# ScalarE in place of GpSimd for the rounding of the middle groups' weights, with VectorE's order changed and the first middle group written out

## The chip, the cores and the metric

The kernel runs on one core of a Trainium2 chip. The metric is the device time of one execution in microseconds (us); the median of three executions is shown, and one more was taken with the hardware profiler. The engines are TensorE (PE, its weight loads PEld), VectorE (DVE), ScalarE (ACT), GpSimd (POOL) and SyncE (SP), which here only issues transfers. All matrices are float32, and each float32 product is made of three passes over two rounded parts (a "high" and a "low" part, both of type float32r).

## The reference, cut to what matters

Two layers work on 1040 tokens (16 of them meta tokens) of width 1024. Each layer is a mixer and then a squared-ReLU MLP with a hidden width of 4096; the change touches only the MLP.

```
def squared_relu_mlp(h, w_up, w_down):
    return jnp.square(jax.nn.relu(h @ w_up)) @ w_down

for l in range(DEPTH):
    mix = hybrid_mixer(rmsnorm(h, norm_mix_pre[l]), w_in[l], ..., w_out[l])
    h = h + rmsnorm(mix, norm_mix_post[l])
    ff = squared_relu_mlp(rmsnorm(h, norm_mlp_pre[l]), w_mlp_up[l], w_mlp_down[l])
    h = h + rmsnorm(ff, norm_mlp_post[l])
return h[:, N_META:]
```

## The kernel before, in words

The hidden width is cut into eight groups of 512. Group 0 and group 7 are computed plainly: four hidden tiles, then eight output tiles. The six groups between them (1 to 6, the middle groups) use Strassen's scheme (in Winograd's form) on 2 x 2 blocks: seven products instead of eight for the up matrix (the **up half** of a group), then seven for the down matrix (the **down half**). The fourteen weight operands of a group are either a quarter of the loaded weights (A11, A12, A22) or a sum of quarters (S1 to S4). In the code they are `UP_A11, UP_S1, UP_S2, UP_S4, UP_S3, UP_A12, UP_A22` and `DN_S4, DN_S3, DN_A11, DN_S1, DN_S2, DN_A12, DN_A22`, and TensorE multiplies them in this order. TensorE's products of the up half are called `UP_1, UP_5, UP_6, UP_3, UP_7, UP_2, UP_4`, those of the down half `X_B22, X_T3, X_B11, X_T1, X_T2, X_B21, X_T4` after their activation operand.

Each weight operand takes these steps. SP loads a quarter of 512 KB into one of four raw buffers (`raws[0..3]`, shown in traces as `w_raw` and `r`), as soon as VectorE has finished with the operand that used the buffer (`when_split`). VectorE makes sums in place (`weights_sum`, L2249). GpSimd rounds the buffer into the high part of one of three weight slots (`rounded`, L679, 128 x 1024 elements; the slots are `w_hl` twice and `w_third`), and VectorE makes the low part (`weights_low`, L2260), after which TensorE may use it.

Beside that, in each middle group, ScalarE copies four up products out of PSUM (`copied`, L1630), squares four hidden quarters (L1634) and rounds the seven activation operands (`high`, L1645); VectorE adds up products (`up_sum`, L2278), applies ReLU and the row scale (`relu`, L2283 and L2360), makes differences (L2287) and low parts of activations (`low`, L2291), and adds down products from PSUM into the output (`add_part`, L2305). SP and ScalarE both issue loads of precomputed activation sums (`t_load`, L543 and L1619; `X<-t_mem`, `t_extra<-t_mem`).

Every engine runs its instructions in the order in which they are written, and waits on semaphores; nothing is scheduled by a tool. In layer 0 a down product has four jobs (tile by tile), in layer 1 two; a job that reuses a PSUM pair waits until VectorE has added the job that was there, and the jobs in the pairs 0 and 2 of layer 0's first down product wait for the last ReLU.

Two more places matter. In group 0, VectorE copies each finished output tile to Y (`down_sum`, L2243), and between two of them makes the second half of the activation sums (`x_sums(1)`, L2437 and L2430; `x_low`, L2447), which ScalarE stores. And at the step from group 0 to group 1, SP loads the quarter A22 of group 1 after group 0's last product, since its buffer lies in the memory of group 0's hidden activations; VectorE then makes two differences on Y (L2465) and the first sum `first_up_sum`.

## Time and profile before

| quantity | value |
|---|---|
| median of 3 runs | 2308.47 us (2308.43 to 2313.3) |
| profiled execution, its time | 2309.11 us |
| profiled execution, its span | 2307.4 us |
| TensorE busy, share of the span | 97% |
| VectorE busy | 72% |
| ScalarE busy | 30% |
| GpSimd busy | 27% |
| mean granted TensorE clock | 0.992 |

The span is the time from the first to the last instruction; 1.7 us lie around it. A busy share tells how much of the span an engine was at work, and not whether its waits matter; the granted clock is 1.0 at 2.4 GHz and 0.5 at 1.2 GHz.

### The profile page before, as it was taken

To read this page: it belongs to the slowest core of one execution; us is meant where nothing else is said; L and a number is where in the kernel's file an instruction comes from. 1 tells how busy PE (TensorE), PEld (TensorE's weight loads), DVE (VectorE), ACT (ScalarE), POOL (GpSimd) and SP (SyncE) were. 2 spreads that over 40 slices of the span, in tenths; PEclk is the share of its full clock that TensorE was granted. 3 is DMA by queue.
4 is the path that set the end of the run, shared out by engine and by line. 5 is a ranking of instruction groups with operands and counts; after the bars stand their busy time and mean duration, and the time that the engine had idled before them with its cause. 6 is when DMAs were issued, how large, how long until landed. Compare 5 with 4: busy or idle time off the path is not lost.

```text
span 2307.4 us, 34577 instructions
## 1 busy us (share of the span) xinstructions
PE 2231.9 (97%) x13856; PEld 2019.0 (88%) x13856; DVE 1651.9 (72%) x1638; ACT 697.7 (30%) x828; POOL 624.5 (27%) x387
## 2 busy tenths in 40 slices
PE   7999999998999999999999999999989999999997
PEld 6999989998999999999989999877777777787787
DVE  6788644665868877977587887354768779778868
ACT  4564433340211211221254653242512112211212
POOL 3333215023222222122414432151232222222240
PEclk9999999999999999999999999999999999999998
DMA  4111002355543554542241111022556544653514
GB/s 136 33 58 39 29 26 89 92 192 209 206 175 136 204 183 155 183 171 77 83 140 46 51 37 37 20 94 80 201 185 225 187 180 152 227 182 122 196 56 146
DMA packets 122673, 290.73 MB, mean 126 GB/s; under 512 B 9552, under 2 KB 29264, under 8 KB 122576
## 3 DMA queue, kind: packets, MB, share of 16 engines
q1 hardware_dynamic: 50032, 153.30, 19.4%
q10 hardware_dynamic: 72544, 136.06, 16.9%
q8 instruction: 70, 1.15, 0.2%
q14 instruction: 27, 0.22, 0.0%
HBM read 251.25 MB, written 38.08 MB: 125 GB/s over the span
## 4 chain that ended last, share of the span: by engine, by line
PE 72%; DVE 14%; issue 5%; DMA 5%; ACT 2%; POOL 1%; DVEq 0%; SPq 0%; POOLq 0%; ACTq 0%
PE banks L802 30%; PE banks L1072 17%; PE banks L1042 9%; PE banks L933 5%; PE banks L854 2%; DMA w_raw<-w_units 2%; DMA r<-w_units 2%; DVE w_hl L2260 2%; POOL w_hl L679 1%; PE banks L857 1%; DVE hid L2278 1%; DVE sum_lo L2291 1%; PE banks L842 1%; PE banks L841 1%; PE banks L1172 1%
## 5 line engine op out<-in xcount | busy, mean ns | idle before, releaser
L802 PE MATMUL banks<-X,w_hl 128*128 128x348 f32 (+2 forms) x3744 | 648.8, 332 | 2.3 <-ACT ki L1558 1.8
L802 PEld LDWEIGHTS banks<-X,w_hl 128*128 128x128 f32 x3744 | 605.7, 188 | 30.2 <-issue 7.5
L1072 PE MATMUL banks<-sum_hi,w_hl 128*128 128x260 f32 (+1 forms) x1440 | 317.4, 325 | 24.4 <-DVE sum_lo L2291 20.0
L1042 PE MATMUL banks<-X,w_hl 128*128 128x260 f32 (+1 forms) x1944 | 316.6, 322 | 7.4 <-DVE w_hl L2260 7.4
L1042 PEld LDWEIGHTS banks<-X,w_hl 128*128 128x128 f32 x1944 | 281.4, 190 | 37.8 <-issue 8.0
L654 POOL TENSOR_SCALAR w_hl<-w_raw 128x1024 fp32r<-128x1024 f32 x70 | 91.7, 1310 | 789.9 <-issue 528.3
L1072 PEld LDWEIGHTS banks<-sum_hi,w_hl 128*128 128x128 f32 x1440 | 227.1, 191 | 53.3 <-issue 26.9
L679 POOL TENSOR_SCALAR w_hl<-r 128x1024 fp32r<-128x1024 f32 x72 | 112.6, 1564 | 361.8 <-DVE r L2249 128.6
L656 POOL TENSOR_TENSOR w_hl<-w_raw,w_hl 128x1024 fp32r<-128x1024 f32 x70 | 201.9, 2885 | 5.8
L1072 PE MATMUL banks<-sum_lo,w_hl 128*128 128x260 f32 (+1 forms) x720 | 192.7, 322 | 0.0
L1630 ACT ACTIVATE hid<-banks 128x1040 f32<-128x1040 f32 (+1 forms) x48 | 49.7, 1035 | 368.8 <-PE banks L1042 368.8
L1645 ACT ACTIVATE sum_hi<-hid 128x1040 fp32r<-128x1040 f32 (+1 forms) x72 | 77.0, 1070 | 253.1 <-PE banks L1072 222.0
L2305 DVE TENSOR_TENSOR Y<-banks,Y 128x520 f32<-128x520 f32 (+1 forms) x144 | 122.0, 867 | 23.5 <-PE banks L1072 23.4
L1072 PE MATMUL banks<-sum_hi,w_third 128*128 128x260 f32 (+1 forms) x576 | 127.3, 321 | 6.4 <-DVE Y L2305 6.4
L1072 PEld LDWEIGHTS banks<-sum_lo,w_hl 128*128 128x128 f32 x720 | 120.5, 191 | 10.0
L679 POOL TENSOR_SCALAR w_hl<-w_raw 128x1024 fp32r<-128x1024 f32 x48 | 55.8, 1162 | 267.7 <-PE banks L1072 216.2
L2260 DVE TENSOR_TENSOR w_hl<-r,w_hl 128x1024 fp32r<-128x1024 f32 x72 | 100.4, 1394 | 22.6 <-POOL w_hl L679 22.6
L1634 ACT ACTIVATE hid<-hid 128x1040 f32<-128x1040 f32 (+1 forms) x48 | 51.3, 1069 | 209.3 <-DVE hid L2283 184.7
L1042 PE MATMUL banks<-X,w_third 128*128 128x260 f32 (+1 forms) x648 | 106.6, 321 | 0.8 <-DMA X<-t_mem 0.6
L1072 PEld LDWEIGHTS banks<-sum_hi,w_third 128*128 128x128 f32 x576 | 90.1, 188 | 16.1 <-DVE Y L2305 7.7
L1042 PEld LDWEIGHTS banks<-X,w_third 128*128 128x128 f32 x648 | 92.4, 188 | 12.1 <-DMA X<-t_mem 2.7
L2249 DVE TENSOR_TENSOR w_raw<-w_raw 128x1024 f32<-128x1024 f32 x24 | 31.5, 1313 | 88.7 <-DMA w_raw<-w_units 88.6
(239 smaller groups left out, 3766.5 us busy)
## 6 DMA issues: line engine op xcount, KB each, us to landing
w_raw<-w_units SPq DMA_DIRECT2D x148, 512.0 KB, 3.5
r<-w_units SPq DMA_DIRECT2D x84, 512.0 KB, 3.8
X<-t_mem ACTq DMA_DIRECT2D x56, 520.0 KB, 6.7
X<-t_mem ACTq DMA_DIRECT2D x56, 512.0 KB, 6.7
X<-t_mem SPq DMA_DIRECT2D x16, 520.0 KB, 5.7
t_extra<-t_mem ACTq DMA_DIRECT2D x16, 520.0 KB, 7.7
X<-t_mem SPq DMA_DIRECT2D x16, 512.0 KB, 5.1
t_extra<-t_mem ACTq DMA_DIRECT2D x16, 512.0 KB, 7.1
```

What stands on the lines that cost most here:

```text
L654: nc.gpsimd.tensor_scalar(slot[:, 0], w_raw[:, s], 1.0, 1.0, ALU.mult, ALU.mult).then_inc(w_rounded, 1)
L656: nc.gpsimd.tensor_tensor(slot[:, 1], w_raw[:, s], slot[:, 0].bitcast(f32), ALU.subtract).then_inc(w_ready, 1)
L679: nc.gpsimd.tensor_scalar(wslots[W_SLOT[operand]][:, 0], raws[raw], 1.0, 1.0, ALU.mult, ALU.mult).then_inc(wpart_hi, 1)
L802: ins = nc.tensor.matmul(out[:, b, 0:t.width(b)], wp, xp[:, t.used(b)], start=first and n == 0, stop=last and n == 2)
L933: ins = nc.tensor.matmul(block_bank(j0, q)[:, 0:t.width(b)], wp, xp[:, t.used(b)], start=i == 0 and n == 0, stop=i == last_k and n == 2)
L1042: ins = nc.tensor.matmul(banks[:, first + b, 0:t.block], wp, xp[:, b * t.block:(b + 1) * t.block], start=opens and (half, kk, i) == (0, 0, ...
L1072: ins = nc.tensor.matmul(out[:, m + b, :], wp, xp[:, k, b * t.block:(b + 1) * t.block], start=k == 0 and i == 0, stop=k == 1 and i == 2)
L1630: nc.scalar.activation(by_up_blocks(l, quarter(l, q)), up_banks(l, chain), ACT.Copy).then_inc(up_copied, 1)
L1634: nc.scalar.activation(quarter(l, q), quarter(l, q), ACT.Square).then_inc(act_sq, 1)
L1645: nc.scalar.activation(sum_part(l, sum_hi, part), source, ACT.Copy).then_inc(xpart_hi, 1)
L2260: V.tensor_tensor(slot[:, 1], raws[W_RAW[operand]], slot[:, 0].bitcast(f32), ALU.subtract).then_inc(wpart_ready, 1)
L2305: ins = V.tensor_tensor(to, part_banks(l, job), to, ALU.add)
```

## The change

1. The rounding of the middle groups' weight operands moves from GpSimd to ScalarE: an ACTIVATE with `Copy` in ScalarE's own order, between its copies, squares and roundings of activations. The operands' GpSimd loop is gone; GpSimd keeps the splitting of all other weights and the zeroing of six tiles.
2. VectorE's up half: the low part of `UP_A12` stands ahead of the wait for the loads of the first down sum; ReLU 1 ahead of the wait for the load of `DN_S4`; the third up sum, the low part of `DN_S4`, ReLU 2 and the low part of `X_B22` ahead of the difference for T3.
3. ScalarE's loads for T3, T4, T2 and T1 follow the roundings that now stand ahead of them.
4. The first middle group stands outside the loop. Its A22 is loaded into a buffer of its own, `r_first`, during group 0's down half; `first_up_sum` is made ahead of group 0's last `down_sum`; the two differences on Y (`spread`) and the wait for the zeroed tiles move behind the low part of `UP_S2`.
5. `x_sums(1)` stands after group 0's second `down_sum` instead of after the first, and its low parts one `down_sum` later.

```diff
+        r_first = at("r_first", [128, 8, 128], A_T3)
...
+                sp.wait_ge(a_lo, FIRST + l * COUNTED_TILES + GT)
+                sp.dma_start(r_first[:, :, :], w_units[l, U_MLP + 8 + Q_A22]).then_inc(raw_loaded[2], 16)
...
                 sp.wait_ge(mm_done, FIRST + done(l, j_down(0, 7)))
-                raw_load(l, 1, 2, 0, Q_A22)
+                raw_load(l, 1, 3, 0, Q_A12)
                 t_load(l, 2, T2, 0)
-                raw_load(l, 1, 3, 0, Q_A12)
...
-                nc.gpsimd.tensor_scalar(wslots[W_SLOT[operand]][:, 0], raws[raw], 1.0, 1.0, ALU.mult, ALU.mult).then_inc(wpart_hi, 1)
...
+                    nc.scalar.activation(wslots[W_SLOT[operand]][:, 0], r_first[:, :, :] if first else raws[raw], ACT.Copy).then_inc(wpart_hi, 1)
...
+                    act.wait_ge(mm_done, FIRST + done(l, j_down(g - 1, 7)))
+                    rounded(g, UP_S1, first)
+                    if first:
+                        act.wait_ge(t_stored, 16 * 20 * (l + 1))
+                    rounded(g, UP_S2)
                     copied(UP_1, 0, (0, 0))
+                    rounded(g, UP_S4)
                     when_half_used(1)
                     t_load(0, T2, 1, (1,))
                     copied(UP_5, 1, (1, 0))
+                    rounded(g, UP_S3)
                     t_load(1, T3, 0)
                     when_half_used(2)
                     t_load(2, T3, 1, (1,))
                     copied(UP_6, 0, (0, 1))
+                    rounded(g, UP_A12)
+                    when_multiplied(UP_3)
+                    rounded(g, UP_A22)
                     t_load(0, T4, 0)
                     square(0, (0, 1))
                     when_half_used(3)
                     t_load(1, T4, 1, (1,))
                     copied(UP_7, 0, (1, 1))
+                    square(1, (1, 1))
+                    rounded(g, DN_S4)
+                    high(X_B22, quarter(l, (1, 1)))
                     if not last:
                         t_load(2, T2, 0)
-                    square(1, (1, 1))
-                    high(X_B22, quarter(l, (1, 1)))
+                    when_multiplied(UP_2)
+                    rounded(g, DN_S3)
+                    square(2, (0, 0))
                     high(X_T3, t3[:, :, 0:HALVES[l].width])
-                    square(2, (0, 0))
-                    square(3, (1, 0))
                     when_half_used(4)
                     when_multiplied(UP_4)
-                    for place in range(2):
+                    rounded(g, DN_A11)
+                    square(3, (1, 0))
+                    for place, (part, source, operand) in enumerate(((X_B11, (0, 0), DN_S1), (X_T1, (0, 1), DN_S2))):
+                        high(part, quarter(l, source))
+                        rounded(g, operand)
                         if not last:
                             t_load(place, T1, place)
                             continue
...
                     weights_low(g, UP_S2)
+                    if first:
+                        spread()
                     weights_low(g, UP_S4)
                     weights_low(g, UP_S3)
+                    weights_low(g, UP_A12)
                     when_loaded(g, 0, 2)
                     when_loaded(g, 1, 2)
                     weights_sum(g, SUM_DN_S1, 1, 0, 1, ALU.add)
-                    weights_low(g, UP_A12)
...
                     if m == KT - 1:
+                        first_up_sum(1, True)
                         weights_low(1, UP_A11)
                     down_sum(m, l * NJ + J_MLP, True)
-                    if m == 0:
+                    if m == 1:
                         x_sums(1)
```

The first place is VectorE in the last middle group of layer 0, from the low part of `UP_S3` (the first row) on; `w_third<-r_97` is the low part of `UP_A12`, `w_raw<-w_raw` the first down sum. Before:

```order
L2260 TENSOR_TENSOR w_hl<-w_raw,w_hl 128x1024
L2249 TENSOR_TENSOR w_raw<-w_raw 128x1024
L2260 TENSOR_TENSOR w_third<-r_97,w_third 128x1024
L2278 TENSOR_TENSOR hid_94<-banks,hid_94 128x2x520
L2283 SCALAR_TENSOR_TENSOR hid_94<-hid_94,rs 128x2x520
```

VectorE at the same place with the change:

```order
L2250 TENSOR_TENSOR w_hl<-w_raw,w_hl 128x1024
L2250 TENSOR_TENSOR w_third<-r_97,w_third 128x1024
L2239 TENSOR_TENSOR w_raw<-w_raw 128x1024
L2269 TENSOR_TENSOR hid_94<-banks,hid_94 128x2x520
L2274 SCALAR_TENSOR_TENSOR hid_94<-hid_94,rs 128x2x520
```

The low part of `UP_A12` moved from behind the down sum, which waits for two loads, to ahead of it.

The second place is VectorE around the end of the same up half, from the second up sum (`hid_95<-hid_95`) to ReLU 3 (`hid_95<-banks,rs`). Before:

```order
L2278 TENSOR_TENSOR hid_95<-hid_95 128x2x520
L2249 TENSOR_TENSOR r_96<-r_96,r_97 128x1024
L2283 SCALAR_TENSOR_TENSOR hid_95<-hid_95,rs 128x2x520
L2260 TENSOR_TENSOR w_hl<-r_96,w_hl 128x1024
L2287 TENSOR_TENSOR t_102<-hid_95,hid_94 128x1040
L2278 TENSOR_TENSOR hid_94<-banks,hid_94 128x2x520
L2291 TENSOR_TENSOR sum_lo_100<-hid_95,sum_hi_98 128x1040
L2283 SCALAR_TENSOR_TENSOR hid_94<-hid_94,rs 128x2x520
L2260 TENSOR_TENSOR w_third<-w_raw,w_third 128x1024
L2360 SCALAR_TENSOR_TENSOR hid_95<-banks,rs 128x2x520
```

VectorE at the same place with the change:

```order
L2269 TENSOR_TENSOR hid_95<-hid_95 128x2x520
L2274 SCALAR_TENSOR_TENSOR hid_95<-hid_95,rs 128x2x520
L2239 TENSOR_TENSOR r_96<-r_96,r_97 128x1024
L2269 TENSOR_TENSOR hid_94<-banks,hid_94 128x2x520
L2250 TENSOR_TENSOR w_hl<-r_96,w_hl 128x1024
L2274 SCALAR_TENSOR_TENSOR hid_94<-hid_94,rs 128x2x520
L2282 TENSOR_TENSOR sum_lo_100<-hid_95,sum_hi_98 128x1040
L2278 TENSOR_TENSOR t_102<-hid_95,hid_94 128x1040
L2250 TENSOR_TENSOR w_third<-w_raw,w_third 128x1024
L2353 SCALAR_TENSOR_TENSOR hid_95<-banks,rs 128x2x520
```

The ten instructions are the same; ReLU 1 stands one place earlier, and the third up sum (`hid_94<-banks`) two places earlier, ahead of the low part of `DN_S4` (`w_hl<-r_96`).

The third place is ScalarE at the start of the same group, from its first instruction of the group on. Before:

```order
L1630 ACTIVATE hid_94<-banks 128x2x520
L1619 DMA X<-t_mem 128x2x520
L1630 ACTIVATE hid_95<-banks 128x2x520
L1619 DMA X<-t_mem 128x2x520 x2
L1619 DMA t_extra_104<-t_mem 128x1040
L1630 ACTIVATE hid_94<-banks 128x2x520
L1619 DMA X<-t_mem 128x2x520 x2
```

ScalarE at the same place with the change:

```order
L1576 ACTIVATE w_hl<-r_96 128x1024
L1576 ACTIVATE w_third<-w_raw 128x1024
L1595 ACTIVATE hid_94<-banks 128x2x520
L1576 ACTIVATE w_hl<-r_96 128x1024
L1584 DMA X<-t_mem 128x2x520
L1595 ACTIVATE hid_95<-banks 128x2x520
L1576 ACTIVATE w_hl<-w_raw 128x1024
L1584 DMA X<-t_mem 128x2x520 x2
L1584 DMA t_extra_104<-t_mem 128x1040
L1595 ACTIVATE hid_94<-banks 128x2x520
L1576 ACTIVATE w_third<-r_97 128x1024
L1576 ACTIVATE w_hl<-r_96 128x1024
```

Six roundings (the rows with `w_hl` and `w_third`) have come between the copies and the transfers; the roundings of `UP_S3` and of `UP_A12` and `UP_A22` stand ahead of the transfers for T3 and T4.

## Rows read from the trace of the kernel before

**Rows 1.** The page: the span.
```profile
span 2307.4 us, 34577 instructions
```
**Rows 2.** TensorE's waits in layer 0's middle groups: releaser, us in total, times, longest.
```profile
PE banks L1072 <- DVE sum_lo L2291: 10.4, 6, 2.8
PE banks L1072 <- DVE Y L2305: 6.4, 6, 1.5
PE banks L1072 <- DVE hid L2360: 4.4, 4, 1.1
PE banks L1042 <- DVE w_hl L2260: 3.7, 1, 3.7
```
**Rows 3.** TensorE's waits in layer 1's middle groups.
```profile
PE banks L1072 <- DVE sum_lo L2291: 9.6, 11, 2.0
...
PE banks L1042 <- DMA X<-t_mem: 0.6, 1, 0.6
```
**Rows 4.** The chain of work in layer 0's group 4: start, us, what.
```profile
817.60 11.49 PE banks L1042 x96
...
831.78 7.44 DMA w_raw<-w_units
...
845.33 4.50 DMA r<-w_units
```
**Rows 5.** Timeline of TensorE, group 4, the start of its down half.
```profile
858.88 0.48 PE L1072 MATMUL banks<-sum_hi,w_hl 128*128 128x260 f32 x2 [1.03 <-DVE sum_lo L2291]
...
863.11 0.51 PE L1072 MATMUL banks<-sum_hi,w_hl 128*128 128x260 f32 x2 [1.11 <-DVE hid L2360]
...
868.37 0.51 PE L1072 MATMUL banks<-sum_hi,w_third 128*128 128x260 f32 x2 [0.66 <-DVE Y L2305]
```
**Rows 6.** Timeline of VectorE, group 4.
```profile
839.24 1.23 DVE L2249 TENSOR_TENSOR w_raw<-w_raw 128x1024 f32<-128x1024 f32 x1 [7.66 <-DMA w_raw<-w_units]
...
853.26 2.06 DVE L2260 TENSOR_TENSOR w_hl<-r,w_hl 128x1024 fp32r<-128x1024 f32 x1 [0.94 <-POOL w_hl L679]
855.24 1.23 DVE L2287 TENSOR_TENSOR t<-hid,hid 128x1040 f32<-128x1040 f32 x1
856.39 1.23 DVE L2278 TENSOR_TENSOR hid<-banks,hid 128x1040 f32<-128x1040 f32 x1
...
859.84 2.06 DVE L2260 TENSOR_TENSOR w_third<-w_raw,w_third 128x1024 fp32r<-128x1024 f32 x1
...
867.63 1.30 DVE L2305 TENSOR_TENSOR Y<-banks,Y 128x520 f32<-128x520 f32 x2
```
**Rows 7.** Timeline of GpSimd, group 4.
```profile
829.27 1.05 POOL L679 TENSOR_SCALAR w_hl<-w_raw 128x1024 fp32r<-128x1024 f32 x1 [2.93 <-PE banks L1042]
...
851.43 1.80 POOL L679 TENSOR_SCALAR w_hl<-r 128x1024 fp32r<-128x1024 f32 x1 [8.93 <-DVE r L2249]
```
**Rows 8.** A group of ScalarE in group 4: busy us, mean ns of one, idle before.
```profile
L1645 ACT ACTIVATE sum_hi<-hid 128x1040 fp32r<-128x1040 f32 x6 | 6.5, 1076 | 22.0 <-PE banks L1072 21.9
```
**Rows 9.** Loads of the tile X in group 4, from issue to landing.
```profile
DMA to landing us min/median/max: 3.9/6.7/8.6
```
**Rows 10.** Timeline of VectorE, from group 0 to group 1 of layer 0.
```profile
517.89 5.04 DVE L2430 SCALAR_TENSOR_TENSOR t_made<-Y,par,t_made 128x520 f32<-128x520 f32 x4
522.85 1.24 DVE L2243 COPY Y<-banks 128x1044 f32<-128x1044 f32 x1
...
554.51 1.25 DVE L2243 COPY Y<-banks 128x1044 f32<-128x1044 f32 x1 [3.34 <-PE banks L802]
...
562.59 1.21 DVE L2260 TENSOR_TENSOR w_hl<-r,w_hl 128x1024 fp32r<-128x1024 f32 x1
```
**Rows 11.** TensorE's waits over the whole span, for group 0's copies alone.
```profile
PE banks L802 <- DVE Y L2243: 4.6, 2, 2.4
```
**Rows 12.** Two stretches: us, busy times of the engines, PEclk, DMA share, GB/s.
```profile
561.00:571.70 10.70, 7.65 (x51) 7.66 (x52) 7.03 (x5) 0.53 (x2) 4.18 (x3) 0.84 0.17 52
...
1716.00:1728.50 12.50, 8.80 (x28) 6.77 (x27) 7.97 (x6) 1.14 (x2) 5.14 (x3) 0.73 0.29 99
```

More of the change, by code:

```diff
@@ L768, in _ @@
                 downs(l, 0, done(l, j_up(0, 2)), done(l, j_up(0, 3)))
-                rounded(l, 1, UP_A11, lambda: pool.wait_ge(mm_done, FIRST + done(l, j_down(0, 5))))
                 pool.wait_ge(t_stored, 16 * 20 * (l + 1))
@@ L1611, in hidden, with rounded, middle_group @@
                     nc.scalar.activation(act_hi[:, i, c], T[2 + i % 2][:, c], ACT.Copy).then_inc(a_hi, 1)
-                def middle_group(g, last):
+                def rounded(g, operand, first=False):
+                    raw, n = W_RAW[operand], groups_before(l, g)
+                    sums = {UP_S1: SUM_UP_S1, UP_S2: SUM_UP_S2, UP_S3: SUM_UP_S3, UP_S4: SUM_UP_S4,
+                            DN_S1: SUM_DN_S1, DN_S2: SUM_DN_S2, DN_S3: SUM_DN_S3, DN_S4: SUM_DN_S4}
+                    loads = {UP_A11: 1, UP_A12: 1, UP_A22: 2, DN_A11: 4, DN_A12: 3, DN_A22: 5}
+                    if operand in sums:
+                        act.wait_ge(wsum_made, WEIGHT_SUMS * n + sums[operand] + 1)
+                    else:
+                        act.wait_ge(raw_loaded[raw], 16 * (RAW_LOADS[raw] * n + loads[operand]))
+                    nc.scalar.activation(wslots[W_SLOT[operand]][:, 0], r_first[:, :, :] if first else raws[raw], ACT.Copy).then_inc(wpart_hi, 1)
+                def middle_group(g, first, last):
                     n = groups_before(l, g)
@@ L1674, in middle_group @@
                             act.dma_start(t_slot(l, place, s).bitcast(f32), b12_part(l, place, s)).then_inc(b12_loaded, 16)
-                    high(X_B11, quarter(l, (0, 0)))
-                    high(X_T1, quarter(l, (0, 1)))
                     high(X_T2, quarter(l, (1, 1)))
+                    rounded(g, DN_A12)
                     high(X_B21, quarter(l, (1, 0)))
+                    rounded(g, DN_A22)
                     high(X_T4, quarter(l, (1, 0)))
+                    if not last:
+                        when_added(6)
+                        rounded(g + 1, UP_A11)
                 w = HALVES[l].width
@@ L2321, in middle_group @@
                     when_summed(g, SUM_UP_S3)
-                    weights_sum(g, SUM_UP_S2, 0, 2, 0, ALU.subtract)
-                    weights_low(g, UP_S1)
+                    V.tensor_tensor(raws[0], r_first[:, :, :] if first else raws[2], raws[0], ALU.subtract).then_inc(wsum_made, 1)
+                    weights_low(g, UP_S1, first)
                     when_loaded(g, 3, 1)
```

101 lines of the change are left out of this document (35 added, 66 removed).

## The prediction, made before the change was run

> **What bounds the kernel now.** I read the page first: the span is 2307.4 us [rows 1], TensorE is busy for 97% of it and VectorE for 72%. So only time in which TensorE waits, or in which it runs at the lower clock, can be won. I then asked for TensorE's waits in the middle groups, because the change touches little else. In layer 0 they sum to 10.4 + 6.4 + 4.4 + 3.7 = 24.9 us [rows 2], in layer 1 to 9.6 + 3.7 + 0.6 = 13.9 us [rows 3], together 38.8 us in twelve groups. Except for 0.6 us, all of them end with an instruction of VectorE. Two more waits, 4.6 us together, one in each layer, are in group 0 on the copy to Y [rows 11].
>
> The next question is what makes VectorE late in a steady group. Take group 4 of layer 0 and count from its first product at 817.60, the group's second 0; a product takes 11.49 / 2 = 5.75 us [rows 4], so the seventh ends at 40.25. TensorE then waits 1.03 us for the low part of `X_B22`, 1.11 us for ReLU 3 and 0.66 us for an addition [rows 5]. VectorE had hardly rested just before these, but it had stood for 7.66 us up to 21.6, waiting for the load of the down quarter A22 [rows 6], which was issued at 14.2 and took 7.44 us [rows 4]. Behind this wait stood the low part of `UP_A12`, whose rounding had long been possible. Two of VectorE's operations also took 2.06 us where their like takes 1.21 [rows 6, 10], and the rounding on GpSimd beside one of them 1.80 where 1.05 is usual [rows 7].
>
> **The change, part by part.** *The rounding.* It is not in the trace on ScalarE, but ScalarE's copy of 1040 elements from SBUF into float32r is: 1.08 us [rows 8]. I take 1.05 to 1.08 for 1024. An undisturbed rounding on GpSimd is 1.05 [rows 7]. The move itself gives nothing, then; what it takes away is the stretching. In group 4 both 2.06 us operations lie in the part of VectorE's queue that TensorE waits for, and each becomes 1.22: 1.7 us. From below this is 0 (the stretching has another cause), from above 1.7; I take 1.7, since GpSimd has no instruction left in the middle groups until the last one ends.
>
> The Trainium skill, "SBUF — State Buffer", section on SBUF's two separate sides, says that VectorE's operations with two SBUF inputs and GpSimd's that read SBUF lock a shared port pair for the whole instruction and block each other. By that rule both sides' stretching goes, as in my sum; without it the 1.7 us stay.
>
> ScalarE's load is no bound: 14 roundings add 15 us to 16 us of work in a group of 84 us. But it is one queue, so I walked through it. At the group's start it rounds `UP_S1` at 0.15 and `UP_S2` at 3.1, before the copy of `UP_1` at 5.8. `UP_S4` follows at 6.9 and ends at 8.0 (TensorE needs it at 17.3). The rounding of `UP_S3` comes after the copy of `UP_5` at 11.5: 12.6 to 13.65, while GpSimd did it from 11.67 to 12.72 [rows 7]. So the low part ends at 15.0 and not 14.0, and the load of down A22 is issued at 15.1. With 7.5 us to landing it is there at 22.6. The transfers for T3, which are now issued after it was rounded (13.7 and 14.3 instead of 11.5 and 12.1), are needed at 23.0; with the median of 6.7 they land at 21.0, with the longest of 8.6 at 22.9 [rows 9]. Those for T4 move from 17.3 to about 24 and are needed at 34.5; with 8.6 they land at 33.1.
>
> *VectorE's order.* The low part of `UP_A12` now runs at 19.5, in the wait. After the landing at 22.6 there are five operations to the second up sum, which cannot start before its copy at 29.9: 22.6 + 1.25 + 1.25 + 1.15 + 1.2 + 2.4 = 29.85, just in time. Then the second up sum, ReLU 1 and the sum for `DN_S4` end at 33.6. The load for that sum is issued at 27.0 and with 4.5 us [rows 4] lands at 31.5, before it is asked for at 32.4. The third up sum waits for `UP_2`, which ends at 34.5. From here VectorE runs without a stop, an operation each 1.15 us (856.39 - 855.24) [rows 6]: the up sum at 34.6, `DN_S4` low 35.7, ReLU 2 36.9, `X_B22` low 38.0 to 39.3, the T3 difference 39.2, `DN_S3` low 40.3, ReLU 3 41.5 to 42.7, `X_T3` low 42.6, two additions 43.8, a difference 45.0, `DN_A11` low 46.15, the third addition 47.3 to 48.0. TensorE needs `X_B22` at 40.25 (1.0 to spare), ReLU 3 at 43.1 (0.4 to spare) and the third addition at 40.25 + 5 x 1.44 = 47.4: it waits 0.6. So layer 0's steady group keeps 0.6 of its 2.8 us, and the six groups 3.6 of 24.9, less the first group's start, told next. In layer 1 the same walk has 0.9 us to spare at `X_B22`, no ReLU is needed for the first product and no addition before the third, so only the 0.6 us on a load stay.
>
> *The first middle group.* TensorE waits 3.7 us there in each layer for the low part of `UP_S1`, which ends at 563.80, 9.3 us after the group's start at 554.5 [rows 2, 10]: the copy, two differences on Y, the first sum, two more sums and the rounding stand in a row. With the first sum made earlier and the differences later the row is: copy to 1.3, two sums to 3.7, low part to 4.9, and TensorE wants it at 5.75. Both waits go, and they are contained in 24.9 and 13.9. The new load of `r_first` has some ten us before anybody asks for it; what hides the differences on Y is the slack of `UP_S4`, needed only at 17.3 and now ready at 10.8. Saved in the middle groups: 24.9 - 3.6 + 13.9 - 0.6 = 34.6 us.
>
> *Group 0.* The copy to Y stands behind `x_sums(1)`, whose last four operations took 5.04 us, and starts only at 522.85 [rows 10], where the tile had been ready since 516.4. With the sums after the second copy the third is asked for at 521.9, gets its turn at about 525, and TensorE needs its banks at 527.6. Both waits go: 4.6 us [rows 11]. The stores of the sums end some 3 us later, and the loads that follow them still have over 10 us.
>
> *The clock.* The granted clock falls to 1.2 GHz after the longest waits: 0.84 over 10.7 us is 1.7 us lost at the start of group 1, 0.73 over 12.5 us is 3.4 us at layer 1's [rows 12]. In layer 0 four such stretches follow the longest waits, of 2.3, 3.7, 2.4 and 2.8 us, in layer 1 three follow those of 3.7 and 2.0 us [rows 2, 3, 11]. That is seven times 1.7 us, 11.9 us at most; since TensorE is still waiting in some of it, I take 1.5 each, 10.4 us. None followed waits of 1.0 to 1.7 us, so with 0.6 us left they should all go.
>
> The sum: 34.6 + 4.6 + 10.4 = 49.6 us. The profiled execution took 2309.1 us with 1.7 us around its span, so 2259.5; the median of the runs shown is 0.6 lower, and I predict **2259 us**.
>
> **The rivals.** *A, the walk holds*: 2259, and as its own range 2253 (the 0.6 us waits go as well, and the clock gives 11.9) to 2266 (the clock gives 7 and the waits lose a further 4). Chance 0.67.
>
> *B, part of the waits stays.* VectorE's chain has no slack at 29.9 and 1.0 us at 34.5, so a landing of down A22 after 23.6 goes through to TensorE one to one. Against it speaks that the transfers for T4 no longer share the engines with this load; for it, that layer 0's ReLU 3 has but 0.4 us. One us more in each of twelve groups is 12 us, and with one or two clock stretches left 3 us: 2274. The case that the stretching was not GpSimd's ends nearby: 1.7 us more in each of six groups is 10 us, 2269. Together 0.27.
>
> *C, the change does not do what it says*: ScalarE's rounding takes in each down product the time that the low parts had. A high part and a rounding in series end 2.2 us after the product before, and their low parts are asked for 5.75 us after it, so I see no way to this; about 2308, chance 0.02.
>
> *D, slower.* The transfers for T4 are issued 7 us later, on ScalarE's queue behind the rounding of `UP_A22`. If they landed after 34.5 + 49.6 / 12 = 38.6, 14 us after the issue, twelve waits would outweigh all gains; with 16 us it would be 12 x 1.9 = 23 us more, 2331. The longest landing in group 4 is 8.6 us [rows 9]. Chance 0.02; a further 0.02 for a slower case that I have not seen.
>
> A rule of the Trainium skill that speaks against the move is in "ScalarE: Activation LUTs", rules for kernel authors: about 0.3 us for each ACTIVATE and 0.83 ns for an element, which would be an estimate of 1.15 us a rounding. By it `UP_S3` would be 0.1 us later than in my walk and the sum 1 us smaller at most; the row of 1.08 decides.
>
> **How the numbers follow.** A has 0.67 and B 0.27; the range takes in both and reaches from **2253 to 2276**. A difference of 0.2%, 4.6 us, is about what a measurement of this kernel can tell from none. A and B lie on the faster side; C and half of the unseen are the same. Faster 0.95, same 0.02, slower 0.03.
>
> **What the profile of the changed kernel would show.** No rounding on GpSimd between group 1 and the last middle group, and ACTIVATEs of 1.05 to 1.08 us in their place; no low part over 1.3 us; a wait of VectorE for the down quarter of about 2 us after the low part of `UP_A12`; TensorE's waits in layer 0's middle groups 3 to 4 us, nearly all on an addition, in layer 1's under 1.5 us; no wait at group 1's start and in group 0; a granted clock of 1.0 from group 0 to the last middle group. I am wrong if TensorE waits on transfers for T3 or T4, if its waits on low parts stay above 1 us a group, or if the clock falls although the waits are short.

## The result, and the profile after

| | before | after |
|---|---|---|
| median | 2308.45 us (4 runs, 2307.14 to 2313.3) | 2252.45 us (4 runs, 2251.06 to 2254.14) |
| ratio | | 0.9754, 95% interval 0.9737 to 0.9771 |
| profiled execution | 2309.11 us, span 2307.4 | 2254.14 us, span 2252.4 |
| mean granted clock | 0.992 | 0.997 |

The change saves 56.0 us. The prediction had the main mechanism (VectorE's order) and the sign, but only 49.6 us, and its range ended 0.55 us above the median measured. The bound was missed by less than the four executions differ, but the sum was short by 6.4 us, and the kernel's second measurement below (2250.8 us) lies outside the range as well.

Among the executions of all experiments below, one of round_only's six was a slow one (3637.82 us, granted clock 0.557); it is left out of that kernel's ratio.

The page of after, its span and its line of busy time:

```profile
span 2252.4 us, 34137 instructions
PE 2215.3 (98%) x13856; PEld 2011.4 (89%) x13856; DVE 1616.8 (72%) x1638; ACT 862.4 (38%) x996; POOL 399.0 (18%) x219
```

TensorE's waits of after over the whole span (us in total, times, longest). These two rows answer to [rows 2, 3]; nothing answers to [rows 11], since no wait on the copies of group 0 is left:

```profile
PE banks L1025 <- DVE Y L2296: 3.3, 6, 0.5
...
PE banks L995 <- DMA X<-t_mem: 0.3, 1, 0.3
```

So 24.9 + 13.9 + 4.6 = 43.4 us of waits became 3.6. To see whether that is all, take the four stages that the change touches: group 0's down half and the middle groups, each in layer 0 and in layer 1. Windows of before, cut at the first and last product of each stage (start:end, us, then busy us of PE, PEld, DVE, ACT and POOL, the granted clock, DMA share, GB/s):

```profile
481.80:554.40 72.60, 70.35 (x433) 70.08 (x434) 43.54 (x37) 21.21 (x20) 22.31 (x15) 0.98 0.56 207
554.40:1072.90 518.50, 493.61 (x4034) 489.35 (x4033) 408.03 (x409) 96.02 (x90) 117.64 (x85) 0.99 0.49 172
1641.20:1710.50 69.30, 66.93 (x290) 53.99 (x289) 43.48 (x37) 20.95 (x20) 22.63 (x15) 1.00 0.58 204
1710.50:2201.30 490.80, 476.71 (x2018) 379.87 (x2017) 396.30 (x325) 94.81 (x90) 117.52 (x85) 0.99 0.51 180
```

The same stages of after:

```profile
483.10:551.70 68.60, 68.60 (x433) 68.60 (x434) 46.05 (x38) 22.28 (x21) 22.36 (x14) 1.00 0.63 227
551.70:1041.30 489.60, 486.30 (x4034) 483.96 (x4033) 388.49 (x408) 177.30 (x173) 3.45 (x2) 1.00 0.51 181
1609.70:1676.40 66.70, 66.70 (x290) 54.09 (x289) 43.84 (x38) 22.00 (x21) 25.16 (x14) 1.00 0.63 222
1676.40:2145.30 468.90, 468.60 (x2018) 378.15 (x2017) 377.79 (x324) 176.10 (x173) 3.46 (x2) 1.00 0.53 187
```

The four stages are shorter by 4.0 + 28.9 + 2.6 + 21.9 = 57.4 us; outside them 2.4 us more than before is spent (1.3 of it ahead of the first stage), which makes the span's 55.0. TensorE did the same matmuls in them and was busy for 1090.2 us instead of 1107.6: 17.4 us of the 57.4 are work that ran faster, the other 40.0 are idle time. The roundings are to be seen too: GpSimd's 118 us in a layer's middle groups became 3, ScalarE's 96 became 177, and VectorE, which has one operation fewer there (1.2 us), is 19.5 and 18.5 us less busy, so 17 to 18 us of stretching are gone in each layer. And the clock column is 1.00 in all four stages.

How a steady group runs now: VectorE in group 4 of layer 0, whose second 0 is 796.59 (start, us, what, idle before and its releaser):

```profile
815.97 1.22 DVE L2250 TENSOR_TENSOR w_third<-r,w_third 128x1024 fp32r<-128x1024 f32 x1 [4.63 <-ACT w_third L1576]
818.37 1.23 DVE L2239 TENSOR_TENSOR w_raw<-w_raw 128x1024 f32<-128x1024 f32 x1 [1.17 <-DMA w_raw<-w_units]
...
831.18 1.24 DVE L2269 TENSOR_TENSOR hid<-banks,hid 128x1040 f32<-128x1040 f32 x1 [1.00 <-PE banks L995]
...
834.63 1.24 DVE L2282 TENSOR_TENSOR sum_lo<-hid,sum_hi 128x1040 fp32r<-128x1040 f32 x1
...
838.07 1.23 DVE L2353 SCALAR_TENSOR_TENSOR hid<-banks,rs 128x1040 f32<-128x1040 f32 x1
...
843.87 1.30 DVE L2296 TENSOR_TENSOR Y<-banks,Y 128x520 f32<-128x520 f32 x2
```

The low part of `UP_A12` starts at 19.4 (19.5 was predicted), the down quarter A22 has landed by 21.8 (22.6), the third up sum starts at 34.6 (34.6), the low part of `X_B22` at 38.0 (38.0), ReLU 3 at 41.5 (41.5), the third addition at 47.3 (47.3). The stop of 7.66 us of [rows 6] is now 4.63 on a rounding and 1.17 on the load, with useful work between them.

TensorE around the only wait left in this group (matmuls in runs of like operands; their ends are modelled):

```profile
843.43 0.40 PE L1025 MATMUL banks<-sum_lo,w_third 128*128 128x260 f32 x2
843.67 0.40 PE L1025 MATMUL banks<-sum_hi,w_third 128*128 128x260 f32 x2
844.61 0.51 PE L1025 MATMUL banks<-sum_hi,w_third 128*128 128x260 f32 x2 [0.55 <-DVE Y L2296]
844.96 0.40 PE L1025 MATMUL banks<-sum_lo,w_third 128*128 128x260 f32 x2
```

It is the predicted wait, 0.55 for 0.6. But these rows show what the prediction left out. Pairs that aren't disturbed start 0.24 us apart. Around the wait, three starts lie 0.94 and 0.35 apart, 0.81 more than two times 0.24, of which the profile calls only 0.55 a wait; 0.26 us are lost beside it. The waits of before show the same, here around the one at 863.11 [rows 5]:

```profile
861.60 0.40 PE L1072 MATMUL banks<-sum_hi,w_hl 128*128 128x260 f32 x2
...
863.46 0.41 PE L1072 MATMUL banks<-sum_lo,w_hl 128*128 128x260 f32 x2
```

The two starts lie 1.86 us apart; two times 0.24 and the wait of 1.11 leave 0.27.

### The profile page after: what moved, and what is told of

It reads as the page before. It is cut to its first block, busy times and chain, and to the rows that moved or that the text cites. A ratio compares the mean times of both kernels' runs of the same rounds, so it can differ in the third digit from the quotient of the medians.

```text
span 2252.4 us, 34137 instructions
## 1 busy us (share of the span) xinstructions
PE 2215.3 (98%) x13856; PEld 2011.4 (89%) x13856; DVE 1616.8 (72%) x1638; ACT 862.4 (38%) x996; POOL 399.0 (18%) x219
## 3 DMA queue, kind: packets, MB, share of 16 engines
q1 hardware_dynamic: 50032, 153.30, 19.5%
q8 instruction: 70, 1.15, 0.2%
## 4 chain that ended last, share of the span: by engine, by line
PE 87%; DVE 8%; ACT 2%; issue 2%; DMA 1%; DVEq 0%; POOL 0%; SPq 0%; ACTq 0%; POOLq 0%
PE banks L755 31%; PE banks L995 19%; PE banks L1025 19%; PE banks L886 5%; PE banks L807 3%; PE banks L810 1%; PE banks L795 1%; PE banks L794 1%; PE banks L1125 1%; PE banks L1132 1%; PE banks L1081 1%; PE banks L1102 1%; PE banks L1203 1%; PE banks L1140 1%; PE banks L924 1%
## 5 line engine op out<-in xcount | busy, mean ns | idle before, releaser
L656 POOL TENSOR_SCALAR w_hl<-w_raw 128x1024 fp32r<-128x1024 f32 x70 | 91.9, 1313 | 1718.3 <-PE banks L1025 954.9
L995 PE MATMUL banks<-X,w_hl 128*128 128x260 f32 (+1 forms) x1944 | 311.7, 320 | 0.0
L1025 PE MATMUL banks<-sum_hi,w_hl 128*128 128x260 f32 (+1 forms) x1440 | 310.9, 320 | 0.0
L1576 ACT ACTIVATE w_hl<-r 128x1024 fp32r<-128x1024 f32 x70 | 73.8, 1054 | 95.3 <-PE banks L1025 45.9
L2296 DVE TENSOR_TENSOR Z<-banks,Z 128x520 f32<-128x520 f32 (+1 forms) x108 | 91.8, 870 | 7.5 <-PE banks L1025 7.4
L2250 DVE TENSOR_TENSOR w_hl<-w_raw,w_hl 128x1024 fp32r<-128x1024 f32 x48 | 58.6, 1220 | 52.0 <-ACT w_hl L1576 52.0
L2282 DVE TENSOR_TENSOR sum_lo<-hid,sum_hi 128x1040 fp32r<-128x1040 f32 (+1 forms) x72 | 88.3, 1226 | 5.1 <-ACT sum_hi L1610 5.1
L2250 DVE TENSOR_TENSOR w_hl<-r,w_hl 128x1024 fp32r<-128x1024 f32 x70 | 85.4, 1219 | 7.2 <-ACT w_hl L1576 7.0
```

What stands on the lines that cost most here:

```text
L656: nc.gpsimd.tensor_scalar(slot[:, 0], w_raw[:, s], 1.0, 1.0, ALU.mult, ALU.mult).then_inc(w_rounded, 1)
L995: ins = nc.tensor.matmul(banks[:, first + b, 0:t.block], wp, xp[:, b * t.block:(b + 1) * t.block], start=opens and (half, kk, i) == (0, 0, ...
L1025: ins = nc.tensor.matmul(out[:, m + b, :], wp, xp[:, k, b * t.block:(b + 1) * t.block], start=k == 0 and i == 0, stop=k == 1 and i == 2)
L1576: nc.scalar.activation(wslots[W_SLOT[operand]][:, 0], r_first[:, :, :] if first else raws[raw], ACT.Copy).then_inc(wpart_hi, 1)
L2250: V.tensor_tensor(slot[:, 1], r_first[:, :, :] if first else raws[W_RAW[operand]], slot[:, 0].bitcast(f32), ALU.subtract).then_inc(wpart_r ...
L2282: V.tensor_tensor(sum_part(l, sum_lo, part), source, sum_part(l, sum_hi, part).bitcast(f32), ALU.subtract)\
```

## The experiments

The first theory, the prediction's: nearly all of the gain is VectorE's place in its queue at each moment when TensorE asks, with 1.7 us a group of layer 0 from the end of the stretching beside GpSimd. The rivals: (1) the rounding's move carries the gain, whatever the order; (2) the 6 us more than predicted are waits and clock stretches that the prediction counted too small; (3) they are a fixed cost that each wait has beside its length. In each comparison "before" is the kernel before, timed on the same chip. The diffs are cut to the lines that matter.

**g0_only.** Part 5 of the change alone.

```diff
-                    if m == 0:
+                    if m == 1:
                         x_sums(1)
```

> The kernel before with one part of the change alone: group 0's second activation sums stand after the second copy to Y, their low parts one copy later. My theory, that each wait of TensorE is a late instruction in VectorE's queue and costs its own length, a little for the restart, and a stretch of halved clock where it is long: both waits in group 0 go (4.6 us), with them the clock stretch in layer 0 (1.7 us) and some 0.5 us of restarts, so 6 to 7 us less than before, about 2302. Rival, that the third copy becomes late instead or the later stores delay group 1: under 2 us less.

Measured 2300.97 us against 2307.26, 0.9967 (0.9955 to 0.9979): 6.3 us, as expected. The two waits are worth 4.6 us by their length, which would leave 1.7 us for what hangs on them; but the interval reaches from 4.8 to 10.4 us, so this rest is not measured well.

**order_only.** Part 2 alone: VectorE's order, with GpSimd still rounding and the first middle group inside the loop.

```diff
                     weights_low(g, UP_S3)
+                    weights_low(g, UP_A12)
                     when_loaded(g, 0, 2)
...
                     up_sum(1, (1, 1), (1, 0))
+                    relu(1, (1, 1))
                     when_loaded(g, 2, 3)
...
-                    relu(1, (1, 1))
...
+                    up_sum(2, (0, 0), None)
                     weights_low(g, DN_S4)
+                    relu(2, (0, 0))
+                    low(X_B22, b22)
```

> The kernel before with VectorE's new order in the up half alone; GpSimd still rounds. My theory: layer 0's steady groups keep about 2.3 us of waits (no wait for the low part of X_B22, 1.3 for ReLU 3 and 1.0 for the third addition, since both stretched operations stay), layer 1's waits at the down half's start go, and with them most clock stretches outside group 1's start: about 20 to 25 us less, near 2286. Rival, that the gain is the end of the port's sharing and the order is worth little: under 8 us less.

Measured 2273.97 us, 0.9855 (0.9841 to 0.9869): 33 us, more than the first theory gave it. TensorE's waits of order_only, whole span:

```profile
PE banks L1042 <- DVE w_hl L2260: 7.4, 2, 3.7
PE banks L802 <- DVE Y L2243: 4.6, 2, 2.4
PE banks L1072 <- DVE Y L2305: 3.7, 6, 0.7
...
PE banks L1072 <- DVE sum_lo L2291: 1.1, 3, 0.4
```

A steady group is as good as after's, though GpSimd rounds. Two of its low parts in group 4:

```profile
843.09 1.25 DVE L2260 TENSOR_TENSOR w_hl<-r,w_hl 128x1024 fp32r<-128x1024 f32 x1
...
847.72 1.21 DVE L2260 TENSOR_TENSOR w_third<-w_raw,w_third 128x1024 fp32r<-128x1024 f32 x1
```

Neither is stretched. GpSimd in the same place:

```profile
841.20 1.05 POOL L679 TENSOR_SCALAR w_hl<-r 128x1024 fp32r<-128x1024 f32 x1 [9.53 <-DVE r L2249]
842.21 1.06 POOL L679 TENSOR_SCALAR w_third<-w_raw 128x1024 fp32r<-128x1024 f32 x1
848.07 1.78 POOL L679 TENSOR_SCALAR w_hl<-r 128x1024 fp32r<-128x1024 f32 x1 [4.80 <-DMA r<-w_units]
```

The first two roundings now fall beside an up sum that reads PSUM (841.93, 1.24 us), and neither side is slower for it. The third falls beside VectorE's low part at 847.72, which has both inputs in SBUF, and there GpSimd takes 1.78 us while VectorE takes its usual 1.21. Before, it was the other way round: VectorE's low part of 2.06 us started at 853.26 [rows 6], just behind a rounding that itself took only 1.05:

```profile
853.20 1.05 POOL L679 TENSOR_SCALAR w_third<-w_raw 128x1024 fp32r<-128x1024 f32 x1
```

In both cases the one that started later took longer, and by about the time that the other still had to run: the low part ends at 847.72 + 1.21 = 848.93, and 1.05 more is 849.98 (the rounding ends at 849.85); the rounding ends at 854.25, and 1.21 more is 855.46 (the low part ends at 855.32). So the two take turns.

The stretching left the part of VectorE's queue that TensorE waits for, so the 1.7 us a group don't need the rounding's move. It did not leave the group: in the same trace VectorE's sums at 807.94 and 812.10 take 1.66 and 1.88 us. VectorE's busy time in layer 0's middle groups is 408.0 us before, 397.6 in order_only and 388.5 with the whole change (one operation fewer), so the order took away 10.5 us of the stretching and the move the last 7.9, which cost TensorE little (see no_round).

**round_only.** The rounding moves to ScalarE with after's order there (parts 1 and 3), VectorE keeps its order.

```diff
-                nc.gpsimd.tensor_scalar(wslots[W_SLOT[operand]][:, 0], raws[raw], 1.0, 1.0, ALU.mult, ALU.mult).then_inc(wpart_hi, 1)
...
+                    nc.scalar.activation(wslots[W_SLOT[operand]][:, 0], r_first[:, :, :] if first else raws[raw], ACT.Copy).then_inc(wpart_hi, 1)
...
```

(`first` is never set in this kernel, so the operand is always `raws[raw]`.)

> The kernel before with ScalarE rounding in place of GpSimd and ScalarE's new order alone; VectorE's order, group 1 in the loop and group 0 are as before. My theory: 1.7 us of stretching and 0.75 us of slower rounding leave VectorE's chain in each group, 1 us is lost because UP_S3 is rounded later; layer 0's groups fall from 2.8 to about 1.4 us of waits and layer 1's nearly to none: 15 to 22 us less, near 2290. Rival, that the order alone gives nearly all: under 5 us less. No VectorE low part should take over 1.3 us in the middle groups.

Measured 2318.18 us over five executions (2319.2 over all six), 1.0048 (1.0035 to 1.0061): 11 us **slower** than before, where both theories had a gain. The sign was missed by all. TensorE's waits of round_only:

```profile
PE banks L1024 <- DVE sum_lo L2279: 35.3, 12, 3.9
...
PE banks L994 <- DVE w_hl L2247: 6.0, 2, 3.0
```

The first row was 10.4 + 9.6 = 20.0 us before [rows 2, 3] and is 35.3 now, in each of the twelve groups. With smaller waits on the ReLUs and on Y (0.8 and 2.0 us) the middle groups' waits are 44.1 us for 38.8, and the mean granted clock is 0.989 for 0.992, some 7 us of the span; the two make the loss. VectorE of round_only in group 4, whose second 0 is 815.84, tells why:

```profile
845.71 1.23 DVE L2236 TENSOR_TENSOR w_raw<-r,w_raw 128x1024 f32<-128x1024 f32 x1 [2.02 <-DMA r<-w_units]
...
849.27 1.22 DVE L2236 TENSOR_TENSOR r<-r,r 128x1024 f32<-128x1024 f32 x1
850.40 1.23 DVE L2271 SCALAR_TENSOR_TENSOR hid<-hid,rs 128x1040 f32<-128x1040 f32 x1
...
853.72 1.23 DVE L2247 TENSOR_TENSOR w_hl<-r,w_hl 128x1024 fp32r<-128x1024 f32 x1 [2.09 <-ACT w_hl L1575]
```

And ScalarE of round_only:

```profile
851.67 1.07 ACT L1598 ACTIVATE hid<-hid 128x1040 f32<-128x1040 f32 x1 [5.92 <-DVE hid L2271]
852.65 1.04 ACT L1575 ACTIVATE w_hl<-r 128x1024 fp32r<-128x1024 f32 x1
```

In the old order ReLU 1 (850.40) stands behind sums that wait for loads. ScalarE stands for 5.92 us before square 1, which needs ReLU 1, and the rounding of `DN_S4` queues behind the square: its sum (849.27) ends at 850.49, the rounding starts at 852.65. Then VectorE waits 2.09 us for this rounding, where it waited 0.94 for GpSimd's [rows 6], which had no square ahead of it. That is 1.15 us of delay. About as much, 1.1 us, comes from a load: VectorE waits 2.02 us at 845.71, where it waited 0.24 before, and the sum for `DN_S4` starts 33.4 us after the group's start instead of 32.3. This load was issued only 0.3 us later in the group than before, but landed 2.0 us later; the transfers for T4 now go out just ahead of it, which is a likely reason and was not tested. The unstretched low part gives 0.8 us back, and the wait for `X_B22` is 2.38 us for 1.03. All low parts take 1.2 us here, so the stretching is gone, and the kernel is slower all the same. This kernel has the new order of ScalarE's loads too, so its 11 us are the price of parts 1 and 3 together.

**first_only.** Part 4 alone (its own buffer for A22, the first sum ahead of group 0's last copy, the differences on Y later), in the old order.

```diff
...
                     if m == KT - 1:
+                        first_up_sum(1, True)
                         weights_low(1, UP_A11)
...
```

> The kernel before with the first middle group outside the loops, its A22 in a buffer of its own, the first sum ahead of group 0's last copy and the differences on Y behind the low part of UP_S2; GpSimd still rounds, VectorE's up half is as before. My theory: the two waits of 3.7 us at group 1's start go, and the clock stretches that follow them (1.7 us in layer 0, 3.4 us in layer 1), so 12 to 13 us less, about 2296. Rival, that GpSimd's stretching (1.9 us operations in this row) keeps UP_S1 late: 1 to 2 us of each wait stay and 3 to 5 us less is gained, about 2300.

Measured 2302.32 us, 0.998 (0.9968 to 0.9992): 5 us, under half of what was expected. The number is the rival's, but not its mechanism: no wait for a weight is left at the group's start. TensorE's waits of first_only in layer 0's middle groups:

```profile
PE banks L1075 <- DVE sum_lo L2295: 8.9, 5, 3.0
```

The window of first_only in which group 1's down half starts (columns as above):

```profile
597.00:607.60 10.60, 8.06 (x54) 8.09 (x55) 10.60 (x11) 3.72 (x4) 2.12 (x2) 0.84 0.47 145
```

The 3.7 us at the group's start are gone, but TensorE then asks 3.7 us earlier for what follows, and the old order is late there anyway: the wait for `X_B22` is 3.0 us for 2.4 before (in layer 1 3.2 for 1.5), the waits on transfers of X are 2.1 us for 0.6, and the clock falls behind both of the longer waits. Of 7.4 us of waits 5.4 were saved (33.4 for 38.8 in the middle groups); the rest was given back half a group later.

**tail_only and a12_only.** The two halves of part 2: the moves around the up sums and ReLUs without the low part of `UP_A12`, and that low part alone.

> The kernel before with the later half of VectorE's new order alone (ReLU 1 ahead of the load for DN_S4, then the third up sum, DN_S4 low, ReLU 2, X_B22 low ahead of the T3 difference); the low part of UP_A12 stays behind the load. My theory: it is this half that matters, since the third up sum can then start as soon as UP_2 ends (34.6 after the group's start) whatever came before, as in the full order: 25 to 33 us less than before, near 2278. Rival, that the low part of UP_A12 in the wait is what counts: under 12 us less.

> The kernel before with the low part of UP_A12 ahead of the load's wait and nothing else. My theory: VectorE's chain comes 0.9 us earlier in each group, layer 0's groups fall from 2.8 to 2.0 us of waits, and one or two clock stretches go: 8 to 15 us less, near 2296. Rival, that the next wait (a load or GpSimd's rounding of DN_S4) takes it all up: under 4 us less.

Measured 2275.78 us, 0.9864 (0.9848 to 0.988), and 2297.91 us, 0.9956 (0.9943 to 0.997), against 2307.28: 31.5 and 9.4 us, both within their expectations. Together they are not worth 41 but 33: they shorten the same chain, and once the tail is in order the `UP_A12` step moves VectorE inside slack. In a12_only's layer 0 the waits on low parts fell from 10.4 us to 1.3 and those on ReLU 3 rose from 4.4 to 6.7, so what is left stands one place further on in the group; in layer 1 the waits on low parts stay (9.5 for 9.6). Both layers:

```profile
PE banks L1072 <- DVE sum_lo L2291: 10.8, 13, 1.8
PE banks L1072 <- DVE hid L2360: 6.7, 6, 1.1
PE banks L1072 <- DVE Y L2305: 4.8, 6, 1.5
```

**no_round.** Everything except the rounding's move and what goes with it: parts 2, 4 and 5, while GpSimd rounds and ScalarE has its old order. It ran beside **after_again**, the changed kernel once more.

> The changed kernel but with GpSimd still rounding in its old loop (first group outside it) and ScalarE's old order: VectorE's new order, the first group and group 0 as changed. My theory now, after the order alone gave 33 us and the rounding alone lost 12: in the new order no low part of TensorE's chain meets a rounding, so the rounding's move is worth next to nothing and this kernel lies within 3 us of the changed one, 2251 to 2256. Rival, the one of my prediction, that 1.7 us of stretching return in each of layer 0's six groups: 8 to 12 us slower than the changed one, 2261 to 2265.

> The changed kernel itself once more, to stand beside the others on the same chip: 2252, with 3.3 us of waits in layer 0's middle groups.

Measured 2252.93 us, 0.9769 (0.9753 to 0.9785), and 2250.8 us, 0.9758 (0.9744 to 0.9773), against 2306.87. The two intervals overlap nearly whole: parts 1 and 3 together are worth about 2 us, and this can't be told from none. Rival (1) falls. no_round's waits:

```profile
PE banks L1075 <- DVE Y L2309: 3.5, 6, 0.7
...
PE banks L1075 <- DVE sum_lo L2295: 2.5, 3, 1.8
...
PE banks L1045 <- DMA X<-t_mem: 1.5, 1, 1.5
```

They sum to 7.5 us for after_again's 3.7; 3.3 us of them are two waits, of 1.5 and 1.8 us, in layer 1's first middle group.

**poke0.** For rival (3): in the changed kernel TensorE, ahead of each of the last six up products, waits for GpSimd, which answers to the product just finished and does nothing else. That is 72 short waits with no other work changed.

```diff
+                with pool.Fori(1, MIDDLE + 1) as g:
+                    for i in range(1, PRODUCTS):
+                        pool.wait_ge(up_done, PRODUCTS * groups_before(l, g) + i)
+                        pool.sem_inc(poked, 1)
...
                 for idx in range(PRODUCTS):
+                    if idx:
+                        pe.wait_ge(poked, 1 * (6 * n + idx))
                     up_product(idx)
```

> The changed kernel with an added handshake: TensorE waits before each of the last six up products of a middle group until GpSimd has seen the product before end (72 short waits, no work in them). It measures what a wait costs beside its own length. My theory from the stage lengths: each shows a gap of 0.1 to 0.3 us in the trace and costs 0.2 to 0.3 us more than its gap, so 22 to 40 us in all. Rival, that a wait costs only its gap: 7 to 20 us.

Measured 2289.41 us, 0.9925 (0.991 to 0.994), 38.6 us over after_again. TensorE's waits of poke0:

```profile
PE banks L1000 <- POOLq L731: 25.4, 72, 0.4
```

TensorE's timeline of poke0, up products of group 4:

```profile
805.00 5.89 PE L1000 MATMUL banks<-X,w_hl 128*128 128x260 f32 x48
811.28 5.98 PE L1000 MATMUL banks<-X,w_hl 128*128 128x260 f32 x48 [0.39 <-POOLq L731]
817.65 3.15 PE L1000 MATMUL banks<-t_extra,w_third 128*128 128x260 f32 x24 [0.39 <-POOLq L731]
...
823.96 6.02 PE L1000 MATMUL banks<-X,w_hl 128*128 128x260 f32 x48 [0.30 <-POOLq L731]
830.35 3.13 PE L1000 MATMUL banks<-X,w_hl 128*128 128x260 f32 x24 [0.38 <-POOLq L731]
```

From 805.00 to 830.35 four products start, 25.35 us where undisturbed ones take 4 x 5.75 = 23.0. The waits shown are 1.46, so 0.89 us, **0.22 for each wait**, is no wait in the profile and yet lost. Over the whole kernel (38.6 - 25.4) / 72 = 0.18, and 0.23 if one counts that the 3.7 us of waits of after_again are gone, since TensorE now comes later. The total was within the expectation; the waits are longer (0.35 us) and what is lost beside them is a little less than the theory had. Rival (3) holds.

**add_first.** Could the last 3.3 us go? The third addition of the down half moves ahead of the T1 difference and the low part of `DN_A11`.

```diff
+                    if t.tiles == 1:
+                        add_part(2)
                     hidden_difference(b12, b12, b11)
                     weights_low(g, DN_A11)
...
-                    add_half(1)
+                    if t.tiles == 1:
+                        add_part(3)
+                    else:
+                        add_half(1)
```

> The changed kernel with layer 0's third addition ahead of the difference and of the low part of DN_A11. My theory, by the walk: the addition may run at 45.0 instead of 47.3, TensorE asks for its bank at 47.4, so the last 0.55 us wait goes in six groups and with it 0.2 to 0.3 us of restart each: 4 to 5 us less than the changed kernel, near 2248. Rival, that the wait moves to the fourth addition or to the third product's operand, now two operations later: under 1 us less.

Measured 2250.28 us, 0.9756 (0.9741 to 0.9772), beside after_again's 2250.8: nothing. In add_first the wait of group 4 stands at the seventh addition instead of the third:

```profile
848.56 0.51 PE L1025 MATMUL banks<-sum_hi,w_hl 128*128 128x260 f32 x2 [0.64 <-DVE Y L2296]
```

VectorE works without a stop from 829.27 to 854.33 in this trace, over all these additions, so this order only chose another place where TensorE waits; no other order was tried.

**s3_plus1 and s3_plus4.** How much slack has ScalarE's queue at the rounding of `UP_S3`? The changed kernel with this rounding done two and five times.

```diff
+                    for _ in range(1):
...
+                        nc.scalar.activation(wslots[W_SLOT[UP_S3]][:, 0], raws[W_RAW[UP_S3]], ACT.Copy).then_inc(extra, 1)
+                        act.wait_ge(extra, 1 * n + _ + 1)
                     rounded(g, UP_S3)
```

> The changed kernel with one more ACTIVATE of the same rounding ahead of UP_S3's, so that its low part, the load of down A22 and the transfers for T3 come 1.15 us later. By the walk the load lands at 21.8 in the changed kernel and may land at 23.6 without harm: within 3 us of the changed kernel, 2250 to 2254. Rival, that the chain through this load has no slack: 12 us more or above.

> The changed kernel with four more such ACTIVATEs, 4.6 us. By the walk the load lands at about 26.4, 2.8 us beyond the bound of 23.6 in layer 0 and 1.9 us beyond layer 1's, and T3's transfers are asked for before they land: 28 us of waits, restarts and some clock stretches, 30 to 50 us more than the changed kernel, 2282 to 2302. Rival, that the slack is larger than the walk says: under 10 us more.

Measured 2253.3 us, 0.9762 (0.9748 to 0.9775), beside after_again's 0.9758: a rounding more costs nothing measurable. With four more, 2276.18 us, 0.9864 (0.9848 to 0.988), some 25 us over after_again, less than the 30 to 50 expected. TensorE's waits of s3_plus4:

```profile
PE banks L996 <- DMA t_extra<-t_mem: 10.7, 12, 1.3
...
PE banks L1026 <- DVE Y L2302: 3.9, 6, 0.7
...
PE banks L1026 <- DVE sum_lo L2288: 2.2, 3, 1.0
```

The down quarter A22 is late as I expected, but what TensorE waits for first is the transfers for T3, which stand behind the roundings in the same queue. This wait comes ahead of the low parts and so takes part of VectorE's lateness off them; I had added up both. In group 4, whose second 0 is 800.56, the low part of `X_B22` starts at 40.2 instead of 38.0, so 2.1 us late; 1.0 us of that is slack, 0.9 is TensorE's own delay by then (a wait of 0.64 and its fixed cost), and the wait there is only 0.31 us.

## Why the prediction was wrong, step by step

**The range failed on the sum.** "The sum: 34.6 + 4.6 + 10.4 = 49.6 us" counts a removed wait at the length that the profile gives it, and has no term for what a wait costs beside it. Against it stands this account of the four stages:

| term | predicted | measured |
|---|---|---|
| waits of the middle groups and of group 0 | 34.6 + 4.6 = 39.2 | 43.4 - 3.6 = 39.8 |
| clock | 10.4 (7 stretches, 1.5 each) | 11.0, at most 7 x 1.7 = 11.9 (none left) |
| what a wait costs beside its length | no term | 25 waits x 0.22 to 0.27 = 5.5 to 6.8 |
| sum | 49.6 | 56.3 to 58.5; the stages show 57.4 |

Before there were 17 + 13 + 2 = 32 such waits, after 7, hence 25. The 0.22 us is poke0's; at the waits themselves the rows at 844.61 and 863.11 show 0.26 and 0.27. The clock was low for 23.9 us in the four stages of before, which is 11.9 us lost if TensorE worked in all of it; it was still waiting in 1.8 us of that (0.1, 0.4 and 1.3 us at three of the stretches), which leaves 11.0. TensorE's busy time gives a check that uses neither price: it fell by 17.4 us with the same matmuls, and less 11.0 to 11.9 for the clock that leaves 5.5 to 6.4 us, or 0.22 to 0.26 for each of the 25 waits. So the step that failed is the missing term, 5.5 to 6.8 us; with it the range would have started near 2247. Rival (2) accounts for the smaller part of the miss: the clock's term was 0.6 to 1.5 us too small, the waits' 0.6.

**The rounding: the arithmetic was right, the cause was not.** The prediction took 1.7 us a group from the stretching's end, "since GpSimd has no instruction left in the middle groups". It did end. But in order_only the low parts that TensorE waits for are unstretched with GpSimd rounding, and no_round is within some 2 us of the changed kernel. The reading behind the 1.7 us had a slip as well: the rounding of 1.80 us at 851.43 [rows 7] ended at 853.23, before the low part of 2.06 us began at 853.26. It stood beside ReLU 1 (851.08, 1.24 us), and the low part stood beside the next rounding, of 1.05 us. "The move itself gives nothing" is true with the new order; with the old one the move and its reordered loads cost 11 us (round_only). This is case C's mechanism, ScalarE's queue, of which I wrote "I see no way to this"; I had looked for it only among the down products, and about half of it sits at `DN_S4`. In the total the error is hidden, because all parts were made together. ScalarE's rounding took 1.054 us (mean of 70) for the assumed 1.05 to 1.08. The rule of the Trainium skill that the prediction used, in "ScalarE: Activation LUTs", rules for kernel authors, gives its 0.3 us for an ACTIVATE whose bias is a pointer operand, which the prediction left out. For one with immediate scale and bias the same page, in "What ACT_TABLE_LOAD costs", has 186 ns and 0.833 ns an element, an estimate of 1.04 us here, and the trace agrees.

The rule of the Trainium skill, "SBUF — State Buffer", section on SBUF's two separate sides, is that of VectorE's operations with two SBUF inputs and GpSimd's that read SBUF, the one that starts first has the shared port pair for its whole instruction and the other blocks. The traces agree: beside an up sum that reads PSUM there was no stretching, and elsewhere the later one took longer by what the earlier still had to run (order_only).

**VectorE's order** was right to 0.1 us at every point of the walk but the landing (21.8 for 22.6, on the safe side). The wait left, 0.55 a group of layer 0, is the predicted one. In layer 1 0.3 us on a load is left for 0.6.

**The first middle group** gave what was said, but only together with the order: alone 5 us, and with the order in place 2273.97 - 6.3 - 2252.93 = 14.7 by difference, if group 0's part is worth its 6.3 us there too. The prediction subtracted both from one list of waits, which is right for the whole; as a price of the part it would have been wrong.

**Group 0**: both waits gone, 6.3 us with what hangs on them (4.8 to 10.4), for the 4.6 and one clock stretch of 1.5 in the sum.

**The clock**: the granted clock is 1.00 in all four stages, as predicted. **Rivals**: B and D did not come; s3_plus1 shows that the slack against B at the quarter A22 is at least one rounding, and s3_plus4 that four use it up. D's transfers for T4 are waited for nowhere.

## What to carry to other kernels

When a busy engine feeds a busier one, walk its queue against each moment when the other asks, and put what is ready into the stops and what is awaited ahead of what isn't: here this order is worth 33 of 56 us, and the first group some 15 more only once the order stands. Moving work to an idle engine moves it into that engine's queue, so ask what stands ahead of it there before you credit it with anything (the same move, with its loads, made the kernel 11 us slower in one order and changed nothing measurable in the other). Price a removed wait at its length, plus a fixed cost measured on the kernel itself (here 0.2 to 0.3 us), plus the lower clock behind it.

## What the runs showed of the hardware that was not expected

- A TensorE wait in these kernels costs 0.2 us and more beside the length that the profile shows (72 waits of 0.35 us in poke0: 0.22 each in the rows, 0.18 to 0.23 over the kernel; 0.26 and 0.27 in the rows of after and before). In the rows it is the overlap with the pair before, and a pair of 0.51 instead of 0.40 us behind it.
- GpSimd's rounding and a VectorE operation that work from SBUF to SBUF take turns: the one that starts later takes longer, VectorE's 2.06 us for 1.21 (before, 853.26) or GpSimd's 1.78 for 1.05 (order_only, 848.07), while the earlier one keeps its time. When VectorE reads PSUM, neither is longer (1.06 and 1.24 in order_only).
- The granted clock fell in or behind waits of 1.8 to 3.9 us in the middle groups (1.81 in first_only, at 854.9), but not behind each of them: after round_only's wait of 3.30 us, up to 2087.9, it stayed at 1.00. It did not fall in poke0's middle groups, whose 72 short waits sum to 25.4 us (mean clock 0.997, as in after).
